# Stage ends of a two-block transformer kernel: order of splits and residuals, four PSUM banks, and a side projection woven into the norm before it

## What is computed

```python
def sqrelu_mlp(hn, w1, w2):
    return jnp.square(jax.nn.relu(hn @ w1)) @ w2
# first program, per layer
h = h + g1 * y                                   # y: mixer or attention output @ w_o
hn = modulate(rms_norm(h, norm2_g[layer]), sh2, sc2)
h = h + g2 * sqrelu_mlp(hn, mlp_w1[layer], mlp_w2[layer])     # d_ff = 4096
# after the first layer: keys and values for all later layers
k, v = split(modulate(rms_norm(h, kv_norm_g), shift, scale) @ kv_w, 2)
# second program, per layer l
x = x + rms_norm_2(y @ w_out[l], norm_post[l])
x = x + jax.nn.sigmoid(x @ w_ple_gate[l]) * (p[l] @ w_ple_proj[l])
```

## Time and profile before

| | |
|---|---|
| three runs | 2713.28, 2717.26, 2717.28 us (median 2717.26) |
| profiled execution | 2714.44 us, of which the span from first to last instruction is 2712.6 us |
| PE busy | 94% of the span |
| DVE, ACT busy | 53%, 41% |
| POOL | four instructions of 0.1 us, none on the data |
| mean granted TensorE clock | 0.967 of full speed |

### The profile page before, as it was taken

How to read it: one execution, slowest core, us unless ns; L and a number is a source line. 1 busy time by engine, 2 the same in 40 slices (tenths; PEclk the granted TensorE clock), 3 DMA queues, 4 the chain that set the end, 5 groups by cost and what they waited for, 6 DMA issues and landing times.

```text
span 2712.6 us, 32170 instructions
## 1 busy us (share of the span) xinstructions
PE 2538.9 (94%) x11846; PEld 2045.7 (75%) x11846; DVE 1445.9 (53%) x2395; ACT 1108.6 (41%) x1956; POOL 0.2 (0%) x4
## 2 busy tenths in 40 slices
PE   3997799999999989999999999999989999999998
PEld 2885688887777768888777777778767777777876
DVE  6777655556656543433446644554354664455435
ACT  3574333333535433433335433333343543343333
POOL 0000000000000000000000000000000000000000
PEclk7999899999999989999989999999998999999999
DMA  5433566666221113223221211222222221122222
GB/s 223 148 109 119 161 216 200 212 197 208 69 86 63 40 64 109 100 94 101 93 93 63 70 63 59 74 71 94 94 70 87 69 70 63 59 74 70 94 93 93
DMA packets 77901, 280.33 MB, mean 103 GB/s; under 512 B 8640, under 2 KB 8896, under 8 KB 77504
## 3 DMA queue, kind: packets, MB, share of 16 engines
q1 hardware_dynamic: 60624, 218.02, 24.2%
q10 hardware_dynamic: 17136, 60.37, 6.9%
HBM read 276.26 MB, written 2.10 MB: 103 GB/s over the span
## 4 chain that ended last, share of the span: by engine, by line
PE 85%; DVE 8%; ACT 4%; issue 2%; ACTq 0%; DMA 0%; DVEq 0%
PE ps L220 24%; PE ps L221 23%; PE ps L222 23%; PE ps L1665 2%; ACT wh L212 1%; PE ps L1579 1%; PE ps L1639 1%; PE ps L1482 1%; PE ps L1013 1%; PE ps L407 1%; DVE bD L276 1%; PE ps L1583 1%; PE ps L1539 1%; PE ps L484 1%; DVE wl L215 1%
## 5 line engine op out<-in xcount | busy, mean ns | idle before, releaser
L215 DVE TENSOR_TENSOR wl<-raw,wh 128x1024 fp32r<-128x1024 f32 x384 | 470.5, 1225 | 928.3 <-ACT wh L212 927.2
L220 PE MATMUL ps<-xh,wl 128*128 128x512 f32 x1728 | 694.1, 402 | 49.4 <-DVE wl L612 24.7
L212 ACT ACTIVATE wh<-raw 128x1024 fp32r<-128x1024 f32 x384 | 405.7, 1057 | 716.1 <-PE ps L222 619.0
L222 PE MATMUL ps<-xh,wh 128*128 128x512 f32 x1728 | 678.1, 392 | 0.0
L221 PE MATMUL ps<-xl,wh 128*128 128x512 f32 x1728 | 677.9, 392 | 0.0
L220 PE MATMUL ps<-bh,wl 128*128 128x512 f32 x1158 | 462.8, 400 | 31.7 <-DVE wl L215 12.5
L221 PE MATMUL ps<-bl,wh 128*128 128x512 f32 x1158 | 456.4, 394 | 0.0
L222 PE MATMUL ps<-bh,wh 128*128 128x512 f32 x1158 | 456.1, 394 | 0.0
L220 PEld LDWEIGHTS ps<-xh,wl 128*128 128x128 f32 x1728 | 326.7, 189 | 167.2 <-issue 53.7
L222 PEld LDWEIGHTS ps<-xh,wh 128*128 128x128 f32 x1728 | 326.9, 189 | 70.1
L221 PEld LDWEIGHTS ps<-xl,wh 128*128 128x128 f32 x1728 | 327.2, 189 | 65.4 <-issue 1.4
(11 more groups left out here) (299 smaller groups left out, 2603.6 us busy)
## 6 DMA issues: line engine op xcount, KB each, us to landing
raw<-in_w SPq DMA_DIRECT2D x388, 512.0 KB, 3.3
bA<-in_ada ACTq DMA_DIRECT2D x74, 512.0 KB, 4.5
bD<-in_ada ACTq DMA_DIRECT2D x16, 512.0 KB, 4.5
bC<-in_ada SPq DMA_DIRECT2D x9, 512.0 KB, 9.7
bS<-in_attn_bias ACTq DMA_DIRECT2D x8, 512.0 KB, 3.3
bC<-in_ada ACTq DMA_DIRECT2D x6, 512.0 KB, 4.1
bD<-in_ada SPq DMA_DIRECT2D x5, 512.0 KB, 14.4
h<-in_x SPq DMA_DIRECT2D x4, 512.0 KB, 9.6
```

What stands on the lines that cost most here:

```text
L212: e.activation(wh[p][:], raw[p][:], ACT.Copy).then_inc(s_hi, 1)
L215: e.tensor_tensor(wl[p][:], raw[p][:], wh[p][:].bitcast(F32), ALU.subtract)\
L220: e.matmul(out, wl[p][:, blk, 0:M], xhi, start=start, stop=False)
L222: return e.matmul(out, wh[p][:, blk, 0:M], xhi, start=False, stop=stop)
```

## The change

- `split_first` and `split_second` are new: the split of units 2 and 3 of a stage is done in two halves of four blocks. The first half may start when PE has passed block 3 of the first pair (event `half0`, `half1`), the second half when the unit before is done. `after_pair` on PE starts unit 2 or 3 on the first halves and waits for the second ones at block 4. Used for the first MLP, `KV`, `O`, and the second MLP.
- Units run over four banks (0 to 3) in the MLPs, in the keys, queries, `O`, `w_out` and the gate.
- For the last two units of an MLP, of `O`, of `w_out` and of the first layer's gate (`end`), ACT and DVE do residual or copy, square and adding ahead of the split. On DVE the down half of the MLP always puts the residual ahead of its part of the split. In the last two steps of the first MLP the `ada` product is put ahead of the residual.
- `rstd_of` takes two hooks that PE runs after `part` and after `sum`: in the second program, the first two of eight steps of the side projection. The other six are issued after the spreading (L431), interleaved in the text with the tiles of the residual. The low parts `xl` of tiles 0 to 6 are made by POOL instead of DVE. The split for the gate's unit 0 is put after tile 5, that for its unit 1 after the last tile.
- The gate's first pair is no longer interleaved tile by tile: unit 0 blocks 0 to 3, unit 1 blocks 0 to 3, unit 0 blocks 4 to 7, unit 1 blocks 4 to 7.

```diff
+            def split_first(u, s, q):
+                p, k = place(u, 0, 0)
+                if act:
+                    e.wait_ge(s_raw[p], 16 * (k + 1))
+                    need(f"{s}half{q}")
+                    done(e.activation(wh[p][:, 0:4, :], raw[p][:, 0:4, :], ACT.Copy), f"{s}wh{q}")
+                if dve:
+                    need(f"{s}wh{q}")
+                    done(e.tensor_tensor(wl[p][:, 0:4, :], raw[p][:, 0:4, :], wh[p][:, 0:4, :].bitcast(F32), ALU.subtract), f"{s}wl{q}")
+
+            def split_second(u):
+                p, k = place(u, 0, 0)
+                if act:
+                    e.wait_ge(s_unit, u - 1)
+                    e.activation(wh[p][:, 4:8, :], raw[p][:, 4:8, :], ACT.Copy).then_inc(s_hi, 1)
+                if dve:
+                    e.wait_ge(s_hi, u + 1)
+                    e.tensor_tensor(wl[p][:, 4:8, :], raw[p][:, 4:8, :], wh[p][:, 4:8, :].bitcast(F32), ALU.subtract).then_inc(s_lo, 1)
+
+            def after_pair(u, bank, used, s, q, hi, lo):
+                if pe:
+                    p, k = place(u, 0, 0)
+                    need(f"{s}wl{q}")
+                    e.wait_ge(s_bank[bank], used + 1)
+                    for kt in range(KD):
+                        if kt == KD // 2:
+                            e.wait_ge(s_lo, 2 * k + p + 1)
+                        mm = mm3(ps[bank][:], p, kt, hi[:, kt, :], lo[:, kt, :], kt == 0, kt == KD - 1)
+                    mm.then_inc(s_unit, 1)
...
                 if pe:
                     need(f"{s}sp{n - 2}")
                     done(sums(sq(n - 2), 6), s + "part")
+                    between[0]()
...
                     done(sums(sq(n - 1), 7), s + "sum")
+                    between[1]()
...
                 if act:
-                    unit_read(u0, it, q)
-                    split(u0 + 2, it, q)
+                    unit_read(u0, 0, m)
+                    if not end:
+                        split(u0 + 2, 0, m)
...
                     if m >= 2:
                         add_square(s + "z", m - 1, zsq)
+                    if end:
+                        split(u0 + 2, 0, m)
...
+                rstd_of(s + "z", KD, D, zsq, (lambda: side(0), lambda: side(1)))
+                if dve:
+                    need(s + "zrstd")
+                for i in range(KD):
+                    q, m = i // 4, i % 4
+                    if pe and i > 1:
+                        side(i)
+                    if act:
+                        if m < 3:
+                            need(f"{n}pp{q}{m}")
+                        else:
+                            unit_read(u0, 0, q)
+                        e.activation(bT[:, i, :], ps[m][:], ACT.Copy).then_inc(s_bank[m], 1)
+                    if dve:
+                        done(e.scalar_tensor_tensor(bC[:, i, :], bC[:, i, :], v("post_g", 8 * l + i), ps[7][:],
+                                                    ALU.mult, ALU.mult), f"{s}n{i}")
+                        need(f"{s}n{i}")
+                        done(e.tensor_tensor(h[:, i, :], h[:, i, :], bC[:, i, :], ALU.add), f"{n}xy{i}")
+                    if act:
+                        need(f"{n}xy{i}")
+                        done(e.activation(xh[:, i, :], h[:, i, :], ACT.Copy), f"{n}xhi{i}")
+                    if pool and i < KD - 1:
+                        need(f"{n}xhi{i}")
+                        done(e.tensor_tensor(xl[:, i, :], h[:, i, :], xh[:, i, :].bitcast(F32), ALU.subtract), f"{n}xlo{i}")
+                    if i == 5:
+                        split(u0 + 2, 0, 0)
+                put_lo(n + "x", KD - 1, hk, None, xh, xl)
+                split(u0 + 2, 0, 1)
```

More of the change, by code:

```diff
@@ new lines, in mlp @@
+                        end = c == N_FF - 1 and n >= 2 * KD - 2
+                        if end:
+                            dots()
+                        if act or (dve and not up):
+                            unit_read(u0, 0, i)
+                        if i < 2:
+                            split_second(u0 + 2 + q)
+                        elif up:
+                            split(u0 + 2, 0, i)
+                        elif act and not end:
+                            split(u0 + 2, 0, i)
@@ L881, in mlp @@
                                 need(f"{ev}mod0")
-                            e.scalar_tensor_tensor(h[:, m, :], ps[q][:], mod[:, g2 + m:g2 + m + 1], h[:, m, :],
-                                                   ALU.mult, ALU.add).then_inc(s_bank[q], 1)
+                            e.scalar_tensor_tensor(h[:, m, :], ps[bk][:], mod[:, g2 + m:g2 + m + 1], h[:, m, :],
+                                                   ALU.mult, ALU.add).then_inc(s_bank[bk], 1)
                         if not up and c == N_FF - 1:
                             m = n - KD
-                            square(nxt, m, hk(m), bTk(m), lambda: e.wait_ge(s_bank[q], b[q] + it + 2))
+                            square(nxt, m, hk(m), bTk(m), lambda: e.wait_ge(s_bank[bk], used + 2))
                             if m >= 2:
                                 add_square(nxt, m - 1, bTk)
[L889 to L899, removed]
+                        if not up and (dve or (act and end)):
+                            split(u0 + 2, 0, i)
+                        if not end:
+                            dots()
                         if dve and up:
@@ L2106, in program @@
                 for m in range(KD):
-                    it, q = m // 2, m % 2
-                    for part, x in ((0, 0), (0, 1), (1, 0), (1, 1)) if pe and m == 0 else ((0, q), (1, q)) if pe and m > 1 else ():
-                        p, k = place(u0, it, x)
+                    bk, used, end = m % 4, b[m % 4] + m // 4, m >= KD - 2
+                    for part, x in ((0, 0), (0, 1), (1, 0), (1, 1)) if pe and m == 0 else ((0, bk), (1, bk)) if pe and m > 1 else ():
+                        p, k = place(u0, 0, m + x if m == 0 else m)
                         if part == 0:
                             e.wait_ge(s_lo, 2 * k + p + 1)
-                            e.wait_ge(s_bank[x], b[x] + it + 1)
+                            e.wait_ge(s_bank[x], b[x] + m // 4 + 1)
                         for kt in range(4 * part, 4 * part + 4):
@@ L2140, in program, with side @@
                 U[0] += KD
[L2141 to L2142 removed]
+                for q in range(4):
+                    BK[q] += KD // 4
                 root_table(s + "z")
[L2144 removed]
                 u0, b = U[0], list(BK)
[L2148 to L2151 removed]
+                def side(i):
+                    q, m = i // 4, i % 4
+                    p, k = place(u0, 0, q)
+                    if m == 0:
@@ L2167, in program @@
-                    split(u0 + 2, 0, q)
+                    if i == 0:
+                        last(n + "p", 2)
+                    e.wait_ge(s_bank[m], b[m] + q + 1)
+                    for kt in range(2):
+                        mm = mm3(ps[m][:], p, 2 * m + kt, bh[:, 1 + kt, :], bl[:, 1 + kt, :], kt == 0, kt == 1)
+                    if m < 3:
+                        done(mm, f"{n}pp{q}{m}")
+                    else:
+                        mm.then_inc(s_unit, 1)
+                rstd_of(s + "z", KD, D, zsq, (lambda: side(0), lambda: side(1)))
@@ L2211, in program @@
                             add_square("L1n", m - 1, bDk)
+                        if end:
+                            split(u0 + 2, 0, m)
                 U[0] += KD
-                for q in range(2):
-                    BK[q] += KD // 2
+                for q in range(4):
+                    BK[q] += KD // 4
                 if l == 0:
```

170 lines of the change are left out of this document (92 added, 78 removed).

## The result

The changed kernel takes 2667.72 us in the median (four runs, 2661.76 to 2668.38), against 2715.27 for the kernel before (four runs, 2712.23 to 2717.28). The ratio is 0.982, 95% interval 0.980 to 0.984. Such a distance is far less than the runs differ among themselves (6.6 us); the question is where the 10 us beyond the forecast came from. The direction was right, the size was not.

A forecast was written before the change was run, and what follows sets the result against it. The prediction took PE, busy 94% of the span, as the bound, with gains only at stage ends and openings. 8.2 + 4.0 + 9.7 + 15.0 = 36.9 us off 2714.44 gave 2677.5, written as 2678; range 2668 to 2694.

The forecast's parts named there:

- Residual ahead of the split: Ends of both MLPs, O, first layer's gate: earlier residual saves 8.2 us, full-clock sums with the hidden split 4.0 more.
- Split in halves: Openings of both MLPs, KV and O: PE's waits behind first pairs shrink, 9.7 us including 1.5 of clock behind O.
- Four banks bring nothing by themselves: Inside a stage: two banks are enough, as neither ACT nor DVE holds PE up; no gain from four.
- Side projection woven in: Second program, `w_out` to gate: side steps between sums and spreading, low parts on POOL; 15.0 us over two layers.
- The root: Behind `w_out`: sums, root and inverse, then spreading of 2.08 us, ending at 1959.9 in the first layer.
- The tile's pace: Residual tiles before the gate: POOL's 1.23 us and DVE's addition of 0.69 exclude each other, 1.92 us per tile.
- case (b): Woven part: POOL and DVE's additions take turns; 15.0 us over both layers, the forecast's choice, chance 0.42.
- The clock: Gate's first pair: a half-clock stretch after PE's idling costs 2.2 us; the 1.6 before unit 2 goes.
- undisturbed DVE (a): Woven part: POOL does not disturb DVE, 1.39 us per tile; 21.8 us there, 2671 in all, chance 0.24.
- POOL first (c): Woven part: addition, rounding, POOL and next addition in one line of 2.6 us; 5.6 us, 2687, chance 0.18.
- little from the ends: Stage ends: sums stay at half clock and DVE's split delays the root; 28.1 us in all, 2686, chance 0.10.
- POOL as bound: Gate's pair waits for POOL's low parts: at 7 us per subtraction 14 us slower, 2728, chance 0.03.

The follow-up runs named there:

- e1_ends: Kernel before with only the stage ends reordered (residual, square and adding ahead of the split; both MLPs, O, first layer's gate): 2702.14 us, ratio 0.9956.
- e8_two_banks: Changed kernel with two banks instead of four in both MLPs, all else kept: 2668.93 us, ratio 0.9839 to the kernel before.
- e3_side: Kernel before with only the second program's `w_out`, side projection and gate as changed, except the gate's end: 2689.72 us, ratio 0.9912.
- e7_no_hooks: Changed kernel without the two hooks in the root, all eight side steps behind the spreading: 2671.95 us.
- the probe: Changed kernel plus five phases behind its last result, timing POOL subtractions and DVE operations alone and together: subtraction 1.23 us alone, 1.67 beside additions.
- e4_early: Changed kernel with the splits for the gate's units 0 and 1 moved forward among the tiles: 2653.77 us, ratio 0.9784 to the kernel before.
- e10_early_no_pool: Changed kernel with those splits moved forward and all low parts made on DVE, POOL without work: 2659.52 us, ratio 0.9788 to the kernel before.

## Why the prediction was wrong

*Residual ahead of the split (8.2 + 4.0)*: right, and for the reason given. The sums of the four ends take 2.25, 1.95, 2.46 and 1.98 us instead of 3.57 or 3.58, at O L423 comes 4.0 us behind PE (4.2 in the working), and `e1_ends` gives 11.5.

*Split in halves (9.7)*: right as a mechanism. The waits of 2.26, 3.08 and 2.26 are gone, KV has 1.53 left where 1.5 was expected. The 1.5 us of clock behind O was not seen back: that stretch gave 5.3 of its 6.9.

*Four banks bring nothing by themselves*: right, as far as the MLPs show (`e8_two_banks`), but they are needed by the openings (2.3 us), which the working took for granted.

*Side projection woven in (15.0)*: this is the step that failed. It measured 24.6 us (the woven stretches' 26.2 less 1.6 for the gate's end), 9.6 more than the term, and `e3_side` alone gave 24.0. Where PE waits, for what and in which order was right. Its terms were mis-sized, each towards too long (the last three points add up for one layer; the first is part of the second):

- The root. I let the spreading take the 2.08 us of rows 5, a half-clock figure, and put the first multiplication 7.3 us behind the last matmul's start. It came at 5.95, 1.35 us earlier. Of that 0.95 is the spreading: PE, kept busy by the hooks, kept full clock and took 1.13. The inverse was done 0.3 earlier. `e7_no_hooks` shows the 2.08 in the second layer when the hooks are gone.
- The tile's pace. Turns on two engines, case (b), are what the probe shows, with 1.23 for POOL as taken; but a pair costs 1.67 and not 1.92, the tile takes 1.70, and that begins at the third tile. The sixth tile was thus added 9.7 us behind the first multiplication, not 11.0. The split beside POOL gave 0.6 back (1.79 instead of 1.23). Unit 0 came at 19.1 and not 21.4, unit 1 at 24.7 and not 27.5: 2.8 us, the root's 1.35 included.
- The order behind. From unit 1 to unit 2, 8.3 us, where the working had 8.2.
- The clock. I charged 2.2 us for a half-clock stretch in the pair. It fell into unit 0's first half (below), and was over before unit 1, for which PE had to wait anyway.

Stretches of the kernel after (columns as in rows 2; the third number from the end is the clock's):

```profile
1951.00:1954.50 3.50, 3.41 (x9) 2.63 (x9) 2.74 (x5) 1.78 (x4) 1.34 (x1) 0.54 0.41 150
1956.70:1965.00 8.30, 8.27 (x36) 6.68 (x36) 1.23 (x1) 2.39 (x3) 0.00 (x0) 1.00 0.19 63
```

So 2.8 + 2.2 = 5.0 of the 4.9 us in the first layer, and the second repeats it (unit 1 at 24.7, unit 2 at 33.2). I should have seen from my own timetable that a slow stretch which ends in a wait costs nothing.

*The range* treated the clock as a loss to be feared only (slow sums) and had 3 us on the fast side. Stretches with the same code differ between these profiled executions with the time at half clock. From the sums of layer 2 to its last matmul of `w_out`, `e4_early` took 592.99 us with 20.5 of them at half clock by the record of granted clocks, the changed kernel 594.59 with 23.9, `e10_early_no_pool` 596.06 with 27.1. That is 3 us, as much as a term of the sum, and the allowance should have stood on both sides.

*Rivals*: undisturbed DVE (a) was wrong in mechanism and would have been closer in size; POOL first (c), little from the ends, and POOL as bound did not happen. Two sums of the working are slightly off: in (a) 1976.9 + 8.2 is 1985.1 and not 1985.4, which puts (a) and with it the fast end of the range some 0.6 us lower, at about 2667.5; and 28.1 us give 2687 and not 2686.

## What to carry to other kernels

At a stage end, look in each engine's queue for work that nobody waits for yet and that stands in front of the one chain on which the busy engine stalls; then look for the place where it costs least, which can be in the middle of the next chain and not at its end, as `e4_early` shows with 11 us. A small amount of work for the matmul engine between dependent steps can be worth more by the clock that it keeps than by being done early, as `e7_no_hooks` suggests with 1 to 2 us per layer. Before a third engine is put on a chain, check whether both it and its neighbour read two operands from SBUF.

## What the runs showed of the hardware that I had not expected

- A POOL subtraction of 128x512 takes 1.23 us alone and 1.67 beside DVE additions with two SBUF inputs; an addition in the residual chain takes 1.01 instead of 0.69, a split of 128x1024 up to 2.27 instead of 1.23. With one DVE input in PSUM the probe shows no effect (1.23 and 0.67 us each).
- The spreading of eight small matmuls took 1.13 us when PE had been busy before it and 2.08 when it had been idle for 1.97 us.
- Profiles of the same code differ by up to 3.1 us in one untouched stretch (592.99, 594.59 and 596.06 us), in steps of some 1.6, with the time at half clock. A difference of one such step between two profiles should not be explained by an edit.
